# A two-layer hybrid trunk: the stored routes read in pieces of 1 KB, sixteen columns to a step

## What is computed

```python
def peer_ffn(h, w_q, sub_keys, u_tab, v_tab):        # 128 tokens at a time
    q = (xb @ w_q).reshape(P_TOKEN_BLOCK, P_HEADS, 2, P_HALF)
    s = jnp.einsum('thcd,ckd->thck', q, sub_keys)
    sv, si = lax.top_k(s, 16)
    ...                                              # 16 of 256 pairs a head: experts, top_s
    g = jax.nn.softmax(top_s, axis=-1)               # 8 heads x 16 experts a token
    a = jax.nn.gelu(jnp.einsum('td,ted->te', xb, u_tab[experts])) * g
    return jnp.einsum('te,ted->td', a, v_tab[experts])
```

## Time and profile before

| | us |
|---|---|
| median of 3 runs | 4631.73 |
| lowest and highest | 4625.6, 4647.27 |
| the profiled execution's own time | 4639.51 |
| span of the profiled execution | 4637.7 |
| TensorE busy | 4104.7 (89%) |
| VectorE busy | 2666.0 (57%) |
| ScalarE busy | 1536.1 (33%) |
| GpSimd busy | 1339.1 (29%) |

### The profile page before, as it was taken

How to read it: one execution, slowest core, us unless ns; L and a number is a source line. 1 busy time by engine, 2 the same in 40 slices (tenths; PEclk the granted TensorE clock), 3 DMA queues, 4 the chain that set the end, 5 groups by cost and what they waited for, 6 DMA issues and landing times.

```text
span 4637.7 us, 62693 instructions
## 1 busy us (share of the span) xinstructions
PE 4104.7 (89%) x18806; PEld 3163.1 (68%) x18806; DVE 2666.0 (57%) x5684; ACT 1536.1 (33%) x2440; POOL 1339.1 (29%) x836
## 2 busy tenths in 40 slices
PE   4877999989998989999848779999899988899998
PEld 2424566659998887777724245666599988777776
DVE  3624331135898867777736242311368998577776
ACT  2324332133443433333323243321334434333332
POOL 0000002124775562222100000021258756522221
PEclk8678989999999999999976789899999999999999
DMA  4300112224678889999633001122247788899996
GB/s 157 136 28 9 46 36 86 73 92 135 225 257 340 311 323 333 337 329 330 229 129 137 16 15 45 37 86 76 89 143 236 262 330 329 332 320 323 335 327 226
DMA packets 334680, 881.63 MB, mean 190 GB/s; under 512 B 27664, under 2 KB 158992, under 8 KB 331024
## 3 DMA queue, kind: packets, MB, share of 16 engines
q1 hardware_dynamic: 220432, 510.08, 32.4%
q0 software_dynamic: 73728, 268.47, 15.2%
q10 hardware_dynamic: 40320, 100.68, 5.6%
HBM read 776.36 MB, written 102.76 MB: 190 GB/s over the span
## 4 chain that ended last, share of the span: by engine, by line
PE 45%; issue 18%; DVE 14%; DMA 13%; POOL 4%; ACT 3%; DVEq 1%; SPq 1%; ACTq 0%; POOLq 0%; PEldq 0%
PE bank L658 12%; DMA W<-tab_v 11%; PE bank L647 6%; PE bank L649 6%; PE bank L648 6%; PE bank L732 3%; PE bank L765 3%; POOL gathered_rows L1388 3%; DVE u_lo L1874 2%; PE bank L706 2%; PE bank L698 1%; PE banks4and L751 1%; DVE arena L1784 1%; DVE gathered_rows L1744 1%; POOL W L1388 1%
## 5 line engine op out<-in xcount | busy, mean ns | idle before, releaser
L1380 POOL TENSOR_TENSOR u_lo<-W,u_hi 128x1024 fp32r<-128x1024 f32 x272 | 694.5, 2555 | 671.5 <-ACT u_hi L1231 667.7
L647 PE MATMUL bank<-h_hi,u_hi 128*128 128x384 f32 (+1 forms) x2176 | 764.2, 351 | 50.7 <-POOL u_lo L1380 45.9
L649 PE MATMUL bank<-h_hi,u_lo 128*128 128x384 f32 (+1 forms) x2176 | 744.0, 342 | 0.0
L648 PE MATMUL bank<-h_lo,u_hi 128*128 128x384 f32 (+1 forms) x2176 | 743.8, 342 | 0.0
L647 PE MATMUL bank<-u_hi,a_hi 128*128 128x512 f32 x1536 | 607.2, 395 | 61.4 <-DVE a_lo L1878 61.4
L1372 POOL TENSOR_TENSOR gate_w_lo<-W,gate_w_hi 128x1024 fp32r<-128x1024 f32 x48 | 115.5, 2409 | 1707.9 <-ACT gate_w_hi L1195 1707.9
L648 PE MATMUL bank<-u_lo,a_hi 128*128 128x512 f32 x1536 | 602.6, 392 | 0.0
L649 PE MATMUL bank<-u_hi,a_lo 128*128 128x512 f32 x1536 | 602.3, 392 | 0.0
L1314 ACT ACTIVATE u_hi<-W 128x1024 fp32r<-128x1024 f32 x256 | 272.5, 1065 | 739.9 <-DMA W<-tab_v 377.3
L647 PEld LDWEIGHTS bank<-h_hi,u_hi 128*128 128x128 f32 x2176 | 416.2, 191 | 62.8 <-issue 36.7
L648 PEld LDWEIGHTS bank<-h_lo,u_hi 128*128 128x128 f32 x2176 | 416.2, 191 | 5.4
(11 more groups left out here) (191 smaller groups left out, 6496.6 us busy)
## 6 DMA issues: line engine op xcount, KB each, us to landing
W<-tab_u SPq DMA_DIRECT2D x256, 512.0 KB
W<-tab_v SPq DMA_DIRECT2D x256, 512.0 KB
W<-stream SPq DMA_DIRECT2D x254, 512.0 KB, 4.5
act_scratch<-act_out ACTq DMA_DIRECT2D x256, 192.0 KB
route_scratch<-arena ACTq DMA_DIRECT2D x24, 2048.0 KB
act_in<-act_scratch SPq DMA_DIRECT2D x64, 768.0 KB
g_cur<-route_scratch SPq DMA_DIRECT2D x64, 768.0 KB
gathered_rows<-u_rows,arena POOLq DMA_INDIRECT x192
```

What stands on the lines that cost most here:

```text
L647: mm(out, w[0], a[0], start=first, stop=False)
L648: mm(out, w[0], a[1], start=False, stop=False)
L649: return mm(out, w[1], a[0], start=False, stop=last)
L1380: nc.gpsimd.tensor_tensor(u_parts[1][:, b, :], raw, u_parts[0][:, b, :].bitcast(F32), ALU.subtract).then_inc(col_lo.sem, 1)
```

## The change

DOWN goes from 8 to 16, so the down loop and that of the sparse sum have 8 steps of 16 columns. g_cur gets two halves of eight columns, twice as large (it takes the place from the unused array "selection"). Its load is issued once in eight columns, ahead of the first V tile of every second set, with runs of 8 x 32 floats, 1 KB; before it SP also waits until the products of the eight columns before that are done (weighted). The activations are loaded for four columns as before, in the same two halves, now four times a step. Waits that count within a step are adapted.

```diff
-DOWN = 8
+DOWN = 16
...
-    "down": (KEYS // DOWN, [0, 1, 2, 3] * 2),
+    "down": (KEYS // DOWN, [0, 1, 2, 3] * (DOWN // 4)),
...
-        g_cur = sb("g_cur", [128, 2, DENSE // TOKENS, 4 * TOKENS])
+        g_cur = sb("g_cur", [128, 2, DENSE // TOKENS, 8 * TOKENS])
...
                 def load_down(step, first=False):
                     for n, slot in enumerate(TILES["down"][1]):
-                        h = n // 4
+                        b = n // 4 % 2
                         if n % 4 == 0:
 
-                            sp.wait_ge(a_lo_done.sem, a_lo_done.at("down", layer, step, n + 4 - DOWN))
-                            sp.dma_start(act_in[:, h].rearrange("p n t -> p (n t)"),
+                            sp.wait_ge(a_lo_done.sem, a_lo_done.at("down", layer, step, n + 4 - 8))
+                            sp.dma_start(act_in[:, b].rearrange("p n t -> p (n t)"),
                                          act_dram[:, ds(step * (DOWN * DENSE) + n * DENSE, 4 * DENSE)]
-                                         ).then_inc(act_loaded[h].sem, 16)
-                            sp.dma_start(g_cur[:, h], route_dram[:, :, ds(step * (DOWN * TOKENS) + n * TOKENS, 4 * TOKENS)]
-                                         ).then_inc(g_loaded[h].sem, 16)
+                                         ).then_inc(act_loaded[b].sem, 16)
+                        if n % 8 == 0:
+
+                            sp.wait_ge(weighted.sem, weighted.at("down", layer, step, n - 8))
+                            sp.dma_start(g_cur[:, n // 8], route_dram[:, :, ds(step * (DOWN * TOKENS) + n * TOKENS, 8 * TOKENS)]
+                                         ).then_inc(g_loaded[n // 8].sem, 16)
...
                     def weigh(step, j):
 
-                        h = j // 4
+                        b, h = j // 4 % 2, j // 8
                         if j % 4 == 0:
-                            dve.wait_ge(act_loaded[h].sem, act_loaded[h].at("down", layer, step, 16))
+                            dve.wait_ge(act_loaded[b].sem, act_loaded[b].at("down", layer, step, 16 * (j // 8 + 1)))
+                        if j % 8 == 0:
                             dve.wait_ge(g_loaded[h].sem, g_loaded[h].at("down", layer, step, 16))
-                        a3 = act_in[:, h, j % 4, :].rearrange("p (g t) -> p g t", t=TOKENS)
-                        tt(a3, a3, g_cur[:, h, :, (j % 4) * TOKENS:(j % 4 + 1) * TOKENS], ALU.mult).then_inc(weighted.sem, 1)
+                        a3 = act_in[:, b, j % 4, :].rearrange("p (g t) -> p g t", t=TOKENS)
+                        tt(a3, a3, g_cur[:, h, :, (j % 8) * TOKENS:(j % 8 + 1) * TOKENS], ALU.mult).then_inc(weighted.sem, 1)
```

More of the change, by code:

```diff
@@ L101 @@
          "rest": 1, "down": KEYS // DOWN,
-         "picked": 3, "early": 3, "routed": 2, "late": 1, "summed": 16}
+         "picked": 3, "early": 3, "routed": 2, "late": 1, "summed": KEYS // DOWN}
 FIRST_COLUMN = {}
@@ L330, in build_trunk @@
         act_in = sb("act_in", [128, 2, 4, DENSE])
-        g_cur = sb("g_cur", [128, 2, DENSE // TOKENS, 4 * TOKENS])
-        assert shared + 16 * DENSE <= shared + 2 * 128 * TOKENS + 2 * HEADS * 256
-        sb("selection", [128, ARENA - shared - (4 * 2 + 8 + 8) * DENSE])
+        g_cur = sb("g_cur", [128, 2, DENSE // TOKENS, 8 * TOKENS])
+        assert shared + 32 * DENSE <= shared + 2 * 128 * TOKENS + 2 * HEADS * 256
+        sb("selection", [128, ARENA - shared - (4 * 2 + 8 + 16) * DENSE])
         gathered_rows = sb("gathered_rows", [128, 6, D])
@@ L445, in build_trunk @@
         h_lo_done = sem("h_lo_done")
-        act_loaded = [signal(f"act_loaded{b}", {"down": 16}, credit=0) for b in range(2)]
+        act_loaded = [signal(f"act_loaded{b}", {"down": 16 * DOWN // 8}, credit=0) for b in range(2)]
         g_loaded = [signal(f"g_loaded{b}", {"down": 16}, credit=0) for b in range(2)]
@@ L452, in build_trunk @@
         rows_ready = sem("rows_ready")
-        sparse_uses = {"early": 8, "routed": Q, "late": 8, "summed": 8}
+        sparse_uses = {"early": 8, "routed": Q, "late": 8, "summed": DOWN}
         row_gathered = [signal(f"row_gathered{b}", {n: 16 * w // GATHERS for n, w in sparse_uses.items()}, credit=0)
@@ L542, in gather_place @@
             for stage, first, steps, width in (("early", 0, 3, 8), ("routed", 24, 2, Q), ("late", 24 + 2 * Q, 1, 8),
[L543 removed]
+                                               ("summed", SPARSE, KEYS // DOWN, DOWN)):
                 if k < first + steps * width:
@@ L626, in _ @@
                 load_down(0, first=True)
-                with sp.Fori(1, 15) as step:
+                with sp.Fori(1, STEPS["down"] - 1) as step:
                     load_down(step)
@@ L632, in _ @@
                     sp.sem_inc(held, 1)
-                load_down(15)
+                load_down(STEPS["down"] - 1)
                 sp.wait_ge(boundary, (layer + 1) * (nstage * 4) + 1)
@@ L1340, in _ @@
                     splits(STEPS["down"] - 1, last=True)
-                    act.wait_ge(row_used.sem, row_used.at("summed", layer, STEPS["summed"] - 1, 8))
+                    act.wait_ge(row_used.sem, row_used.at("summed", layer, STEPS["summed"] - 1, DOWN))
                     act.sem_inc(held, 1)
@@ L1850, in sparse_down @@
                         landed = row_gathered[j % GATHERS]
-                        dve.wait_ge(landed.sem, landed.at("summed", layer, step, 16))
+                        dve.wait_ge(landed.sem, landed.at("summed", layer, step, 16 * (j // GATHERS + 1)))
                         dve.wait_ge(row_used.sem, row_used.at("summed", layer, step, j))
-                        stt(pair[:], gather_slot(j), weight[:, ds(step * 8 + j, 1)], pair[:], ALU.mult, ALU.add
+                        stt(pair[:], gather_slot(j), weight[:, ds(step * DOWN + j, 1)], pair[:], ALU.mult, ALU.add
                             ).then_inc(row_used.sem, 1)
                     def weigh(step, j):
-                        h = j // 4
+                        b, h = j // 4 % 2, j // 8
                         if j % 4 == 0:
-                            dve.wait_ge(act_loaded[h].sem, act_loaded[h].at("down", layer, step, 16))
+                            dve.wait_ge(act_loaded[b].sem, act_loaded[b].at("down", layer, step, 16 * (j // 8 + 1)))
+                        if j % 8 == 0:
                             dve.wait_ge(g_loaded[h].sem, g_loaded[h].at("down", layer, step, 16))
-                        a3 = act_in[:, h, j % 4, :].rearrange("p (g t) -> p g t", t=TOKENS)
-                        tt(a3, a3, g_cur[:, h, :, (j % 4) * TOKENS:(j % 4 + 1) * TOKENS], ALU.mult).then_inc(weighted.sem, 1)
+                        a3 = act_in[:, b, j % 4, :].rearrange("p (g t) -> p g t", t=TOKENS)
+                        tt(a3, a3, g_cur[:, h, :, (j % 8) * TOKENS:(j % 8 + 1) * TOKENS], ALU.mult).then_inc(weighted.sem, 1)
                     def split(step, last_step=False):
                         for j in range(DOWN):
-                            a = act_in[:, j // 4, j % 4, :]
+                            a = act_in[:, j // 4 % 2, j % 4, :]
                             if j + 1 < DOWN:
@@ L1884, in _ @@
                     split(STEPS["down"] - 1, last_step=True)
-                    dve.wait_ge(row_used.sem, row_used.at("summed", layer, STEPS["summed"] - 1, 8))
+                    dve.wait_ge(row_used.sem, row_used.at("summed", layer, STEPS["summed"] - 1, DOWN))
                     dve.sem_inc(held, 1)
```

2 lines of the change are left out of this document (1 added, 1 removed).

## The result

The changed kernel takes 4778.85 us (median of 6 runs, 4743.0 to 4792.74), the kernel before 4628.66 (6 runs, 4608.39 to 4647.27). The ratio is 1.0311, interval 1.0279 to 1.0342: slower, as forecast, but by 150 us where the forecast said 70, and above the end of its range (4750). The profiled execution of the changed kernel took 4792.74 us with a span of 4790.9.

The account below looks back on a forecast made before the run. TensorE was taken as the floor, with waits for first V tiles. Pairs of sets at 37.5 us gave +73 us, less at most 3 for loop turns: +70 on 4639.5, said as 4700; range 4595 to 4750 for 8 in 10.

Parts of the forecast that it names:

- TensorE as the floor: In the down part TensorE's own matmuls set the floor: 32.66 us per eight columns, against 34.83 and 35.32 really taken.
- the first tile of a set as the wait: Once in four columns TensorE waits, through a_lo, for the set's first V tile, queued behind activations and routes.
- only set A waiting: Of each eight columns, set A (with route load) would idle 3.05 us; set B (without), latency 8.4, not at all.
- Idle time is latency minus 10.15: For a set issued on time, TensorE idles by its first V tile's latency, issue to u_hi's start, less 10.15 us.
- 1.6 us of slow matmuls behind a wait over 2 us: After idle time beyond 1.96 us TensorE's clock halves; about eight matmuls are slow, adding 1.6 us.
- 50 ns for a 1 KB piece: Assumed DMA price of a 1 KB route piece, bounds 41.5 and 57.8, against 28.9 ns for 512 B.
- Rival 3: 1 KB route pieces cost like two of 512 B: latency 14.0, idle 3.85, time 4725; chance 0.12.
- No cost of SP's new wait, of the loop and of code loading: SP's wait for weighted adds nothing; fewer loop turns save at most 3 us; no instruction-fetch stall in TensorE's down loop.
- rival 4: TensorE's doubled down loop stalls for code at its branch, up to 6250 ns: +75 us, 4775; chance 0.04.
- A: 11.2 + 2.0 = 13.2, idle 3.05: Set A's first V tile: latency 11.2 us plus 2.0 for the larger route load ahead, so TensorE idles 3.05.
- The base of 11.2: First V tile's latency before the change for a set issued on time, taken midway between 10.37 and 12.07 us.
- Rivals 1 and 2: Set A's wait stays under the clock's edge: about 4610, chance 0.15; set B's relief makes it faster: 4592, chance 0.22.

Follow-up runs that it names:

- e11: Steps of 16 columns, 768 KB of routes per set in 512 B pieces, issued behind the third V tile of the set ahead, no wait for weighted: 4559.59 us, 0.9819.
- e12: As e11, but 1 KB pieces, each load taking half of the token groups for eight columns: 4567.78 us, ratio 0.9828 to the kernel before.
- e3: The changed kernel with its 1 KB route load split in two by token groups, 768 KB ahead of every set's first V tile: 4639.77 us, 1.0011.
- e1: The changed kernel with routes loaded for four columns again in 512 B pieces, only the loop longer: 4636.51 us, ratio 1.0014 to the kernel before.
- e8: The kernel before without the gathers of V rows and the wait for them: 4556.59 us, ratio 0.9803.
- e6: The changed kernel without the gathers of V rows and the wait for them: 4555.74 us, ratio 0.9798 to the kernel before.
- e2: The changed kernel with its one route load of 1 KB pieces cut into two of 512 B pieces at the same place: 4798.55 us, ratio 1.0358.
- e9: The changed kernel with its 1536 KB route load issued from ScalarE's own DMA queue behind columns 3 and 11, without the wait for weighted: 4706.53 us, 1.0133.
- e15: The kernel before with its 768 KB route load per set issued from ScalarE's own DMA queue: 4589.77 us, ratio 0.9871.

## Why the prediction was right in sign and short in size

Step by step:

- **TensorE as the floor, the first tile of a set as the wait, and only set A waiting: right.** A's tiles have a latency of 15.9 us, and B's cause no wait. B's latency was forecast as 8.4 and came out at 9.6, still inside the margin.
- **Idle time is latency minus 10.15: right.** It gives 16.61 - 10.15 = 6.46 for the set shown, which had 6.36, and 5.8 for the mean latency, where 5.7 was measured.
- **1.6 us of slow matmuls behind a wait over 2 us: right in kind, a little short.** The 26 sets A that waited 2.9 us or more lost 1.5 to 2.5 us behind it, 2.1 on average. In these sets the loss at the 1.2 GHz level does not grow with the wait: 1.5 us behind the wait of 8.26, 2.5 behind one of 3.97.
- **50 ns for a 1 KB piece: right within the rows.** A stretch with hardly anything but such pieces, 4448 to 4450, has

```profile
q1 hardware_dynamic: 493, 0.53, 81.6%
```

which is 2 x 16 x 0.816 / 493 = 53 ns; over both down parts the 1 KB pieces take 51 on average. The bound of two 512 B pieces, 57.8, is not reached. Rival 3 (double cost) is out by this row, and e11 against e12 shows no price of the piece size either. By the Trainium skill, page "DMA: Bandwidth & Descriptors", section Specifications, 512 B would already be enough for the line rate; the trace does not agree, it has 17.7 B/ns there and 1024/53 = 19.3 here, against 24.7 for gathered rows.

- **No cost of SP's new wait, of the loop and of code loading: right**, by e3 for the wait, by e1 for the loop, and by TensorE's branch of the new down loop, which has at most 233 ns (rival 4 needed 6250):

```profile
L1031 PEldq COMPARE_BRANCH  x12: 76/208/233, 1901.9 to 4700.4; - x12
```

- **The term that failed: "A: 11.2 + 2.0 = 13.2, idle 3.05".** The latency was 15.9 us and the idle time 5.7. I added the burst's own extra time, 2.0 us, to a latency, as if the tile's queue had the engines to itself. The size of that time was right for engines without gathers: the tile lands after 6.9 us in e8 and 8.9 in e6, 2.0 later. With the gathers, which take a third of the engines, it comes 5.5 later. The DMA rows above have the parts in one set: +2.9 for SP's queue, +2.6 for gathers, 0.8 for gaps; over all sets they are 2.9, 2.0 and 0.6. The base of 11.2 was taken too high, which hid a part of the error: sets with 768 KB ahead have 10.4 (e1, e3), and 15.9 is 5.5 above that.

With the measured latency in the prediction's own sum, a pair is 32.66 + 5.8 + 1.6 + 0.16 = 40.2 us, and (40.2 - 34.83 + 40.2 - 35.32) x 15 - 3 = 151: 4639.5 + 151 = 4790.5, where the profiled execution took 4792.74. So one term explains the miss. That the sum then fits within 2 us is partly luck. With the measured 5.7 and 1.9 for idle time and slow matmuls a pair is 40.4 us and the sum some 6 us more. And from TensorE's first to its last matmul the two down parts grew by 160 us (556.6 to 656.2 and 564.1 to 624.9), while all else together took 7 us less.

Rivals 1 and 2 rested on a latency of A under 12.1 and 12.0; in the change this holds for 2 of the 28 sets A, whose pairs took 34.4 us; the mean is 15.9. What they saw right is the price of the two small waits: e11 and e12 take them away and gain 1.8%, 70 to 80 us, about the 75 us that the prediction called the most that the change could touch.

What stays open: why SP's own transfers grow by more than the pieces do. The pieces explain 1536 x (53 - 28.9) / 16 = 2.3 of the 2.9 us in the set shown. Over all sets, from the tile's issue to its u_hi, packets of V tiles take 3.4 us of 16 engines instead of the 2.5 of the kernel before, though a tile is the same; in e6, with the same burst and no gathers, it is 2.6. That would fit engines that get out of step when burst and gathers meet, some already at the next tile while the last one still owes pieces of this one. No experiment here separates it.

## What to carry to other kernels

A load is priced by what stands behind it, and its own engine time is only a lower bound of that price while other queues use the same engines: here 768 KB more ahead of a tile, in pieces of twice the size, cost 2.0 us without the gathers and 5.5 with them. Dividing by the share that the gathers leave is not enough either: 2.0 over two thirds is 3.0. Halving the number of loads by doubling each one here halved the waits and made them more than five times as long (from 0.7 and 1.0 us to 5.7), so where the margin (here 10.15 us) is small, many small loads did better than few large ones. Better still is to move the load to a place where nothing urgent follows. The size of the pieces was worth nothing that could be measured: at a bad place 512 B and 1 KB gave 1.0358 and 1.0311, at a good one 0.9819 and 0.9828.

## What the runs showed of the hardware that was not expected

- Two loads in a row of 1536 pieces each held SP for 6.72 us at their issue in one set of e2, and for 4.8 us in the median of its 32 bursts; the one load of 1536 pieces in the changed kernel holds it for 0.59 us.
- A transfer on a queue of its own still delays those of another. A first tile, with 768 KB of activations ahead in its queue, lands 12.5 us after its issue with 1536 KB begun beside it (e9), and 9.4 and 8.9 us after it (sets A and B) with 768 KB begun beside it (e15). In e9 itself, first tiles with no burst begun beside them (set B) land after 6.4.
- The gathers, 30% of the DMA engines' time in the down part, cost the kernel before 2.0% (e8), most of it through the wait of the first tile: e11 gets 1.8% back with all gathers in place.
